# A hybrid diffusion step on one core: one pair of adaLN gates of the last layer computed as VectorE dot products in place of TensorE products

## What is computed

```
for i, mixer in enumerate(layers):                 # cond: c_ctx for context, c for latent tokens
    shift1, scale1, gate1, shift2, scale2, gate2 = split(silu(cond) @ ada_w[i] + ada_b[i])
    h = rmsnorm(x) * (1 + scale1) + shift1
    x = x + gate1 * mixer(h)
    h = rmsnorm(x) * (1 + scale2) + shift2
    x = x + gate2 * (silu(g) * val) @ w_down       # g, val = split(dwconv(h @ w_up))
```

## Time and profile before

| | us |
|---|---|
| median of 3 runs (lowest, highest) | 1865.88 (1864.75, 1870.98) |
| the profiled execution | 1867.3 |
| its span, first to last instruction | 1865.5 |
| TensorE busy | 1806.4 (97%) |
| VectorE busy | 1340.8 (72%) |
| ScalarE busy | 981.5 (53%) |
| chain that ended last: TensorE's share | 87% |
| TensorE's mean granted clock | 0.993 |
| loads from memory | 405 MB, 223 GB/s over the span |

### The profile page before, as it was taken

The page is one execution under the profiler, slowest core; times in us unless marked ns, Lnnn a source line. Parts: engine busy times, 40 slices in busy tenths (PEclk is TensorE's granted clock), DMA queues, the critical chain, the costliest instruction groups (busy, mean ns, idle before and its releaser), DMA issues.

```text
span 1865.5 us, 27382 instructions
## 1 busy us (share of the span) xinstructions
PE 1806.4 (97%) x11100; PEld 1499.6 (80%) x11100; DVE 1340.8 (72%) x1973; ACT 981.5 (53%) x1470; POOL 178.8 (10%) x154
## 2 busy tenths in 40 slices
PE   5999999999999989999999999999999999999998
PEld 2988777797888867888977678888888786878888
DVE  2865677668897566998655688966764776769984
ACT  1754344545674354766344466744653445447763
POOL 2100121001000113000011110002100210020001
PEclk8999999999999999999999999999999999999999
DMA  8565656867655757665574776556555647645542
GB/s 350 207 226 194 201 206 226 316 229 285 248 181 191 276 207 291 248 243 185 197 297 166 295 279 261 188 184 249 226 183 185 231 175 282 242 159 203 189 177 87
DMA packets 72527, 418.12 MB, mean 224 GB/s; under 512 B 12176, under 2 KB 18696, under 8 KB 24144
## 3 DMA queue, kind: packets, MB, share of 16 engines
q1 hardware_dynamic: 54288, 392.98, 56.4%
q10 hardware_dynamic: 18112, 23.38, 3.9%
HBM read 405.35 MB, written 10.95 MB: 223 GB/s over the span
## 4 chain that ended last, share of the span: by engine, by line
PE 87%; DVE 6%; DMA 2%; ACT 2%; issue 2%; POOL 1%; POOLq 0%; SPq 0%; DVEq 0%; ACTq 0%
PE ps L586 18%; PE ps L606 9%; PE ps L641 9%; PE ps L589 9%; PE ps L568 6%; PE ps L622 5%; PE ps L644 4%; PE ps L571 3%; PE ps L683 3%; PE ps L554 3%; PE ps L556 3%; PE ps L555 3%; DMA raw<-in_stream 2%; DVE spl_lo L471 2%; PE ps L890 1%
## 5 line engine op out<-in xcount | busy, mean ns | idle before, releaser
L471 DVE TENSOR_TENSOR spl_lo<-raw,spl_hi 128x1024 fp32r<-128x1024 f32 x556 | 686.9, 1258 | 189.0 <-ACT spl_hi L460 188.2
L460 ACT ACTIVATE spl_hi<-raw 128x1024 fp32r<-128x1024 f32 x556 | 574.2, 1053 | 301.0 <-PE ps L644 111.0
L586 PE MATMUL ps<-H,spl_hi 128*128 128x512 f32 x1408 | 443.9, 397 | 3.6 <-DVE H L1756 3.6
L589 PEld LDWEIGHTS ps<-H,spl_lo 128*128 128x128 f32 x1408 | 264.5, 188 | 62.4
L589 PE MATMUL ps<-H,spl_lo 128*128 128x256 f32 x1408 | 276.7, 278 | 0.0
L586 PEld LDWEIGHTS ps<-H,spl_hi 128*128 128x128 f32 x1408 | 214.3, 189 | 14.9 <-issue 14.8
L641 PE MATMUL ps<-G,spl_hi 128*128 128x512 f32 x528 | 165.8, 395 | 0.0
L568 PE MATMUL ps<-B,spl_hi 128*128 128x512 f32 x512 | 160.9, 395 | 0.0
L554 PE MATMUL ps<-H,spl_hi 128*128 128x256 f32 x512 | 147.9, 289 | 6.7 <-DVE H L1756 5.2
L556 PE MATMUL ps<-H,spl_lo 128*128 128x256 f32 x512 | 145.9, 285 | 0.0
L555 PE MATMUL ps<-H,spl_hi 128*128 128x256 f32 x512 | 145.9, 285 | 0.0
(11 more groups left out here) (248 smaller groups left out, 2894.9 us busy)
## 6 DMA issues: line engine op xcount, KB each, us to landing
raw<-in_stream SPq DMA_DIRECT2D x374, 1024.0 KB, 4.9
out_new_C<-c_stage ACTq DMA_DIRECT2D x16, 512.0 KB, 6.2
ada_b<-in_ada_b ACTq DMA_DIRECT2D x4, 768.0 KB, 9.4
E<-rows_out ACTq DMA_DIRECT2D x8, 256.0 KB, 4.3
Em<-rows_out ACTq DMA_DIRECT2D x8, 256.0 KB, 4.6
x<-in_x ACTq DMA_DIRECT2D x1, 1024.0 KB, 12.0
wide<-rows_out ACTq DMA_DIRECT2D x8, 128.0 KB, 4.7
cache<-in_na_cache ACTq DMA_DIRECT2D x1, 1024.0 KB, 8.3
```

Source lines behind the costliest of these rows:

```text
L460: act.activation(spl_hi[m % SPL][:, :], raw[r % RAW][:, h * HALF:(h + 1) * HALF], ACT.Copy).then_inc(S["hi_done"], 1)
L471: dve.tensor_tensor(spl_lo[m % SPL][:, :], raw[r % RAW][:, h * HALF:(h + 1) * HALF], spl_hi[m % SPL][:, :].bitcast(F32), ALU.subtract).the ...
L586: pe.matmul(banks[:, b * 512:(b + 1) * 512], spl_hi[m % SPL][:, c], H[:, kk * 512:(kk + 1) * 512], start=kk == 0, stop=False, skip_group_c ...
L589: mm = pe.matmul(banks[:, b * 512:b * 512 + TOK], spl_lo[m % SPL][:, c], H[:, kk * 512:kk * 512 + TOK], start=False, stop=kk == KD - 1, sk ...
```

## The change

The eight `ada` tiles of layer 3's phase 1 leave TensorE. In their place eight tiles `ada_column` hold the same weights the other way round: each has 128 output channels on the partitions and 1024 inputs for each of the two gates. A dot product along the row with the condition vector, present on every partition (`cond_all`), gives the gate's column at once. Four such tiles stand in the stream within `ffn_down` of layer 1 and four within that of layer 2, behind tiles 2, 4, 6 and 8; c0 to c3 below. VectorE makes four dot products from each (two gates, two conditions): two at the end of the splits of each round from 2 to 9. Each waits for the one before it, since they write the same `product`. A column tile is released by its fourth dot product. ScalarE makes SiLU of the conditions as rows at the start, writes them to memory and reads them back to all partitions within the FFN's first product (1 MiB, in layers 1 and 2). The fills of layer 3 fall from 3 to 2 (`CONV_FILL`) and from 2, 2, 2, 1 to none (`HEAD_FILL`). With phase 1 go one `copy_mod`, one `mod_rows` and one `mod_columns`; two small additions of the bias take their place. The number of tiles in the stream is the same.

```
-CONV_FILL = {0: 3, 3: 3}
+CONV_FILL = {0: 3, 3: 2}
-HEAD_FILL = {0: [2, 3, 3, 2], 3: [2, 2, 2, 1]}
+HEAD_FILL = {0: [2, 3, 3, 2], 3: [0, 0, 0, 0]}
+COLUMN_LAYER = 3
+COLUMN_AT = [2, 4, 6, 8]
...
-        order += [("ffn_down", i, t) for t in range(11)]
+        for t in range(11):
+            order.append(("ffn_down", i, t))
+            if i in (1, 2) and t in COLUMN_AT:
+                order.append(("ada_column", COLUMN_LAYER, 4 * (i - 1) + COLUMN_AT.index(t)))
...
                 if last[0] == "ada":
                     sp.wait_ge(S["ada_used"], INDEX[last] + 1)
+                elif last[0] == "ada_column":
+                    sp.wait_ge(S["dot_done"], 4 * INDEX[last] + 4)
                 else:
                     sp.wait_ge(S["lo_done"], 2 * INDEX[last] + 2)
...
-                    if t == 3 and i:
-                        mod_rows(i, 1)
...
+                    if j == 6 and i in (1, 2):
+                        act.wait_ge(S["condr_kept"], 16)
+                        act.dma_start(cond_all[:, :], cond_out.rearrange("a b -> (a b)").unsqueeze(0)
+                                      .to_broadcast([P, NS * D])).then_inc(S["conda_landed"], 16)
...
+            act.dma_start(cond_row[:, :], io["cond_rows"]).then_inc(S["condr_landed"], 16)
+            act.wait_ge(S["condr_landed"], 16)
+            act.activation(cond_row[:, :], cond_row[:, :], ACT.Silu).then_inc(S["condr_silu"], 1)
+            act.wait_ge(S["condr_silu"], 1)
+            act.dma_start(cond_out, cond_row[:, :]).then_inc(S["condr_kept"], 16)
...
+            def dot(g, n):
+
+                r = POS["ada_column", COLUMN_LAYER, g]
+                landed(dve, r)
+                dve.wait_ge(S["conda_landed"], 16 * (g // 4 + 1))
+                for s in range(NS):
+                    o, done = (n * KD + g) * NS + s, 4 * g + 2 * n + s
+                    if done:
+                        dve.wait_ge(S["dot_done"], done)
+                    dve.scalar_tensor_tensor(product[:, :], raw[r % RAW][:, n * D:(n + 1) * D], 1.0,
+                                             cond_all[:, s * D:(s + 1) * D], ALU.mult, ALU.mult,
+                                             accum_out=dots[:, o:o + 1]).then_inc(S["dot_done"], 1)
...
                 for t in range(begin, count):
                     split_lo(dve, n0 + t + 1)
                     if t == begin and columns is not None:
                         columns()
+                    if dots_of is not None and 2 <= t <= 9:
+                        dot(4 * dots_of + (t - 2) // 2, t % 2)
                     for pair in ends_pair(nk, t):
...
-                if i:
-                    copy_mod(i, 1)
...
                     if g == 2 and i:
-                        mod_columns(i, 1)
+                        dve.wait_ge(S["dot_done"], 32)
+                        for n, coef in enumerate(coef_g):
+                            link(dve.tensor_tensor(v3(coef[:, :], NS), v3(dots[:, n * KD * NS:(n + 1) * KD * NS], NS),
+                                                   sc("ada_c", n * KD, KD).unsqueeze(2).to_broadcast([P, KD, NS]), ALU.add))
```

More of the change, by code:

```diff
@@ L62 @@
           ("ml_conv_w", 2 * 3 * KI), ("ml_conv_b", 2 * KI), ("ml_norm_w", 2 * KI), ("ml_skip", 2 * KI),
-          ("n0", 2 * 16), ("m0", 2), ("b_gate", 2), ("sink", NH), ("final_w", KD), ("cond", 2 * KD)]
+          ("n0", 2 * 16), ("m0", 2), ("b_gate", 2), ("sink", NH), ("final_w", KD), ("cond", 2 * KD), ("ada_c", 2 * KD)]
 COL = {}
@@ L83, in stream_order @@
     order = []
-    adas = iter([("ada", i, g) for i in range(DEPTH) for g in range(ADA_TILES)])
+    adas = iter([("ada", i, g) for i in range(DEPTH) for g in range(ADA_TILES)
+                 if (i, g // ADA_PHASE) != (COLUMN_LAYER, 1)])
     def fill(count):
@@ L150, with mod_index @@
 ADAS = [tile for tile in ORDER if tile[0] == "ada"]
-MAIN = [tile for tile in ORDER if tile[0] != "ada"]
-INDEX = {tile: n for tiles in (MAIN, ADAS) for n, tile in enumerate(tiles)}
+COLUMNS = [tile for tile in ORDER if tile[0] == "ada_column"]
+MAIN = [tile for tile in ORDER if tile[0] not in ("ada", "ada_column")]
+INDEX = {tile: n for tiles in (MAIN, ADAS, COLUMNS) for n, tile in enumerate(tiles)}
+def mod_index(i, phase):
+    return 3 * i + phase - ((i, phase) > (COLUMN_LAYER, 1))
 def chunked(w, k0, nk, c0, nc):
@@ L191, in host_tile @@
         return np.concatenate([rows[:, v * D:(v + 1) * D] for v in MOD_SOURCE[2 * p:2 * p + 2]], 1)
+    if kind == "ada_column":
+        o = P * tile[2]
+        return np.concatenate([w["ada_w"][i][:, v * D + o:v * D + o + P].T for v in MOD_SOURCE[2:4]], 1)
     if kind == "ml_x":
@@ L266, in host_arrays @@
     put("cond", np.stack([columns(w["c_ctx"]), columns(w["c"][0])], 2).reshape(P, 2 * KD))
+    put("ada_c", np.concatenate([columns(w["ada_b"][COLUMN_LAYER].reshape(6, D)[v]) for v in MOD_SOURCE[2:4]], 1))
     ada_b = np.zeros((DEPTH, 4, 32, 3, ADA_N), f)
@@ L274, in host_arrays @@
         "stream": stream, "small": small,
+        "cond_rows": np.concatenate([w["c_ctx"].reshape(-1), w["c"][0].reshape(-1)]).reshape(16, P).astype(f),
         "x": np.concatenate([w["x_prompt"][0], w["x_sample"][0]], 0).T.reshape(KD, P, TOK).transpose(1, 0, 2)
@@ L339, in build @@
     ow = [sb(f"ow{b}", 2 * TOK, F32, rW + 4 * KB + 2 * KB * b) for b in range(2)]
+    cond_all = sb("cond_all", NS * D, F32, rB + 12 * KB)
+    product = sb("product", D, F32, rB + 20 * KB)
+    cond_out = nc.dram_tensor("cond_out", (16, P), F32, kind="Internal").ap()
     RB = sb("RB", 2 * TOK, F32, rW)
@@ L388, in build @@
     ccol = small_sb("ccol", NS * 36)
+    dots = small_sb("dots", 2 * KD * NS)
+    cond_row = small_sb("cond_row", P, rows=16)
     gI, gF, gA, gM, gb, gc, gG = (small_sb(n, TOK) for n in ("gI", "gF", "gA", "gM", "gb", "gc", "gG"))
@@ L427, in build @@
     names = """raw0 raw1 raw2 raw3 hi_done lo_done half_used
-        loads x_loaded cond_silu cond_zero cond_done ada_used misc_init
+        loads x_loaded cond_silu cond_zero cond_done ada_used dot_done condr_landed condr_silu condr_kept conda_landed misc_init
         adab_landed modb_done modT_mm modT_done
@@ L678, in ada @@
                 r = POS["ada", i, g]
-                if k == 0 and 3 * i + phase:
-                    pe.wait_ge(S["modT_done"], 3 * i + phase)
+                if k == 0 and i + phase:
+                    pe.wait_ge(S["modT_done"], mod_index(i, phase))
                 landed(pe, r)
@@ L695, in mod_rows @@
             def mod_rows(i, phase):
-                pe.wait_ge(S["modb_done"], 3 * i + phase + 1)
+                pe.wait_ge(S["modb_done"], mod_index(i, phase) + 1)
                 for b in range(4):
@@ L1657, in _ @@
                 if i + 1 < DEPTH:
-                    act.wait_ge(S["modb_done"], 3 * i + 3)
+                    act.wait_ge(S["modb_done"], mod_index(i, 2) + 1)
                     act.dma_start(ada_b[:, :], io["ada_b"][i + 1]).then_inc(S["adab_landed"], 16)
@@ L1685, in mod_columns @@
             def mod_columns(i, phase):
-                dve.wait_ge(S["modT_mm"], 3 * i + phase + 1)
+                dve.wait_ge(S["modT_mm"], mod_index(i, phase) + 1)
                 if phase != 1 and link.n:
@@ L1694, in mod_columns @@
                 if phase != 1:
-                    dve.wait_ge(S["modT_done"], 3 * i + phase + 1)
+                    dve.wait_ge(S["modT_done"], mod_index(i, phase) + 1)
                     nw = sc("norm_w", (2 * i + phase // 2) * KD, KD)
@@ L1772, in norm, with project @@
                 h_lo(3)
-            def project(n0, count, nk, r, begin=0, columns=None):
+            def dot(g, n):
[9 more added lines that the diff above has]
+                                             accum_out=dots[:, o:o + 1]).then_inc(S["dot_done"], 1)
+            def project(n0, count, nk, r, begin=0, columns=None, dots_of=None):
                 for t in range(begin, count):
@@ L2282, in ffn @@
                                          .to_broadcast([P, KD, NS])))
-                project(INDEX["ffn_down", i, 0], 11, 2 * NJ, 2 * i + 1, 1)
+                project(INDEX["ffn_down", i, 0], 11, 2 * NJ, 2 * i + 1, 1,
+                        dots_of=i - 1 if i in (1, 2) else None)
             for k, name in enumerate(("conv_done", "xc_lo", "z_mul", "z_lo")):
```

## The result

The changed kernel takes 1908.15 us (median of 4 runs, 1906.95 to 1909.23) where the kernel before takes 1866.6; the ratio is 1.0221 (95% interval 1.0208 to 1.0233). It is 41.5 us slower; 1903 was forecast, with a range of 1892 to 1917. The profiled execution has a span of 1905.1 us, 39.6 more than before.

The account below looks back on a forecast made before the run. TensorE, busy 97% of the span, was taken as the bound. Two layers of 19.8 + 2 us less 6.4 gave +37.2 on 1867.3, 1904.5; the profiled execution being 1.4 above the median, 1903, range 1892 to 1917.

Parts of the forecast that it names:

- The loop: FFN's second product, layers 1 and 2: load, splits and dots take 15.7 us per two tiles, TensorE needs 11.2.
- The recurrence: Layer 2's product followed release by release: waits of 3.8, 4.5, 4.5 and 2.2 us before tiles 5, 7, 9, 10.
- the wait for `H`: Middle of the mixer's first product: TensorE's earlier wait disappears, 0.9 us less loss a layer.
- the sum: Whole kernel: two layers of 19.8 us plus 2 for the clock, less 6.4 gained, +37.2 us.
- The clock: Norm behind the product: TensorE's short work between waits runs at a lower clock, 2 us a layer, 0 to 3.5.
- The price of a dot: VectorE's 128x1024 dot products in layers 1 and 2: 1.3 us each, 2.6 a pair, range 1.23 to 1.5.
- Rival 1: VectorE's dots run at half rate, 2.3 us each, 29 us more, 1932; chance 0.08.
- The gain: Last layer's mixer: 5.7 us from three heads, 0.3 behind the first products, 0.4 from transposes; 6.4 us.
- Rival 4: Last layer's heads: the removed tiles cover something unseen, so nothing is won, 1909; chance 0.04.
- The cheap places: Start and broadcasts: ScalarE's squares begin near 18.9 instead of 13.17, covered by 2.3 us; cost 0.
- Rival 2: Layers 1 and 2: the ring doesn't hold TensorE, c0 released 3.8 us earlier, 1859.5; chance 0.04.
- Rival 3: Layers 1 and 2: loads come in time and only VectorE's sum of work counts, 1871; chance 0.04.

Follow-up runs that it names:

- e1: Changed kernel with its dot products reading a resident row and each column tile given back on landing; 1865.37 us.
- e5: Changed kernel with all four dot products of a column tile in the first of its two rounds (2, 4, 6, 8); 1877.44 us.
- e10: Changed kernel with 14 spare TensorE products before tiles 5, 7 and 9 of the FFN's second product in layers 1 and 2; 1905.56 us.
- e11: As e10, with 14 more spare products before the first `ada` tile of the norm behind the product; 1908.95 us.
- e2: Changed kernel with each dot product over 64 elements instead of 1024, column tiles kept as long as before by the same waits; 1880.33 us.
- e3: Changed kernel without the eight column tiles, the 32 dot products and the broadcasts; 1860.83 us.

## Why the prediction was right, and where it was off

**The loop.** The recurrence was followed on layer 2's own clock. Offsets in us from the product's first instruction:

| | forecast | layer 1 | layer 2 |
|---|---|---|---|
| c0 given back | 24.7 | 24.6 | 24.6 |
| tile 5 starts | 31.8 | 31.8 | 31.7 |
| tile 7 starts | 47.5 | 46.9 | 48.4 |
| tile 9 starts | 63.2 | 63.4 | 64.9 |
| c3 given back | 74.7 | 76.1 | 77.6 |
| product ends | 76.9 | 77.6 | 78.5 |
| first `ada` tile of the norm | 79.4 | 81.2 | 82.5 |
| mixer starts | 90.4, and 2 for the clock | 94.2 | 94.3 |

The mechanism, its place and, within 10%, its size are as forecast, and e1 and e5 show that it is the kept buffer. The net loss a layer, with the wait for `H` in the mixer that is gone, was 23.7 and 23.9 where 21.8 was forecast. For that wait the sum took 0.9 us where its row has 0.67. The single waits came out shorter than forecast (3.8 and 2.3, 3.7 and 3.7 before tiles 5 and 7, where 3.8 and 4.5 were worked out) because TensorE's slower instructions fill part of the loop's time; the loop's length is what was forecast.

**The step that was short.** c3 is given back 1.4 and 2.9 us later than forecast, because the sum took all of VectorE's instructions at their mean. Beside GpSimd's sums of squares, three of them in each layer take longer: the dot at 1281.77 (2.31 instead of 1.22, had no row for it), the split at 1303.59 (3.45 for two halves instead of 2.36), and the dot at 1306.96 (1.76). These are 2.7 us on the path in layer 2, and the same three stand in layer 1. VectorE's and GpSimd's timelines of layer 2:

```profile
1303.59 3.45 DVE L493 TENSOR_TENSOR spl_lo<-raw,spl_hi 128x1024 fp32r<-128x1024 f32 x2
1306.96 1.76 DVE L1814 SCALAR_TENSOR_TENSOR product<-raw,cond_all 128x1024 f32<-128x1024 f32 x1
...
1308.76 1.23 DVE L1814 SCALAR_TENSOR_TENSOR product<-raw,cond_all 128x1024 f32<-128x1024 f32 x1
```

```profile
1281.01 2.00 POOL L2388 TENSOR_TENSOR sqa<-sq,sq 128x512 f32<-128x512 f32 x1 [173.27 <-ACT sq L1232]
1303.75 2.21 POOL L2388 TENSOR_TENSOR sqa<-sqa,sq 128x512 f32<-128x512 f32 x1 [20.74 <-ACT sq L1232]
1306.10 1.54 POOL L2388 TENSOR_TENSOR sqa<-sqa 128x256 f32<-128x256 f32 x1
```

In layer 1 the loop from tile 5 to tile 7 was 0.5 us shorter than forecast (15.2), in layer 2 1.0 longer (16.7), since the load of tile 7 landed after 6.1 us and not after 4.6; why is open.

**The clock.** I gave the norm 2 us a layer for it, and nothing for the product. In the traces TensorE's instructions took 5.0 us more in each product and 4.0 more in each norm. e10 puts the first at 0.4 and 0.95 by the product's end and at 1.7 and 0.2 by the mixer's start, 1 us a layer and near to the nothing of the forecast, and in e11 the second can't be shown to cost anything. So my 2 us were wrong in kind; by luck they stood for the 2.7 us of the three slow instructions, and without them the forecast would have been 1899. Where no late loads hide it this may be otherwise: in e1 TensorE's slower instructions are 1.9 of the 2.7 us more in layer 2's norm, and no run shows what a higher clock would give back there.

**The price of a dot.** 1.22 us and 0.08 for the accumulator, 1.27 from one dot to the next, 2.5 a pair; 1.3 was taken. Rival 1 is out: 28 of the 32 took 1.22 to 1.23 us. Half the rate, as the Trainium skill (Vector Engine (DVE) Microarchitecture Reference, section 7, Points that are easy to get wrong) has it for two SBUF sources that aren't bf16, would be 2.3 us, so the rule doesn't hold for this operation on this chip; the four that took 1.8 to 2.3 are explained by GpSimd. It would not have been without effect: between e2 and the changed kernel the four dots of a column grow from 1.0 to 5.0 us, and that costs 28 us for the eight columns.

**The gain.** 6.4 forecast, 6.5 in the traces, 5.7 between the medians of e3 and the kernel before. In its parts: TensorE now waits 1.15 us for `mod_b` behind the fourth head, where it waited 0.18, and 0.63 for the low part behind the first products, of which the forecast had 0.5. Rival 4 is out.

**The cheap places.** ScalarE squares from 18.82 on (18.9 forecast), and TensorE takes the sums at 26.67 (26.72 before). Cost 0, as forecast:

```profile
18.00 0.31 ACT L1673 ACTIVATE cond_row<-cond_row 16x128 f32<-16x128 f32 x1 [8.85 <-DMA cond_row<-in_cond_rows]
...
18.82 1.13 ACT L1232 ACTIVATE sq<-x 128x512 f32<-128x512 f32 x2
```

**The other rivals.** Rival 2 needed c0 given back 3.8 us earlier; it came when forecast. Rival 3, only VectorE's work counts, is e1: it put the result near 1871, and e1 measured 1865.4, since not even the residuals make TensorE wait. The real cost of the work is in the norm.

What the forecast of e2 missed, 19.5 for 4 to 9 us, goes with three things: the clock and GpSimd, in a version where no loop hides them, and in layer 1 the load of tile 9 that landed late. Which of them has what part was not measured apart.

## What to carry to other kernels

In a ring that is filled in order, price a tile by how long it keeps its buffer and by who stands behind it, not by the work that is done on it: the same 32 dots cost 47 us or nothing, by their round. Here it paid to do the work on an inserted tile in one piece, in a round that has nothing else, and not just ahead of a stretch that takes many tiles in a short time. Before adding VectorE work with two SBUF inputs, look where GpSimd runs.

## What the runs showed of the hardware

- A scalar_tensor_tensor of 128x1024 with two SBUF sources in fp32 and a sum takes 1.22 us, as much as a plain subtraction of that size (1.22 alone), and 0.08 for the accumulator.
- Beside a GpSimd addition of 128x512 in SBUF, such a dot takes up to 2.3 us. GpSimd's own 128x256 addition takes 1.54 instead of 0.74 us where it begins beside a split. In the changed kernel and the eight others with full dots, all 26 dots that began while a GpSimd addition ran took longer, and none of the other 254 did (1.23 us at most).
- Residuals with a source in PSUM that run beside GpSimd (at 733.10 and 1097.09 in the changed kernel) show nothing of this: 0.34 us each in either case.
- The mean granted clock of the product fell from 1.00 to 0.93 when TensorE had to wait in it. In the changed kernel it ran at its lower level, 1.2 GHz, for a few us behind each of the four waits of 3.7 to 4.7 us (two products of 128x512 took 1.06 us instead of 0.63, as below from layer 2), and stayed at 1.00 behind the three of 1.6 to 2.5. The length of the wait alone doesn't settle it: in e2 the clock stayed at 1.00 behind a wait of 1.79 us in layer 1 and fell behind one of 1.86 in layer 2 (0.80 over the 8.6 us that followed). In e10, 3.4 us of spare products in each of the waits before tiles 5, 7 and 9 held it at the higher level.

```profile
1266.93 1.06 PE L665 MATMUL ps<-G,spl_hi 128*128 128x512 f32 x2
...
1269.97 0.63 PE L665 MATMUL ps<-G,spl_hi 128*128 128x512 f32 x2
```
